# Solving 16x16 instead of 8x8 diagonal blocks on VectorE in the triangular inverse of a gated DeltaNet kernel

## The reference

```python
kb = kc * bc[..., None]
lower = jnp.tril(jnp.einsum('...id,...jd->...ij', kb, kc) * decay, -1)
a_mat = lower + jnp.eye(c, dtype=f32)
rhs = jnp.concatenate([vc * bc[..., None], kb * jnp.exp(gcum)[..., None]], axis=-1)
sol = lax.linalg.triangular_solve(a_mat, rhs, left_side=True, lower=True, unit_diagonal=True)
...
attn = jnp.einsum('...id,...jd->...ij', qc, kc) * decay
def step(s, xs):
    u_i, w_i, attn_i, qg_i, kg_i, gl_i = xs
    v_new = u_i - jnp.einsum('nhck,nhkv->nhcv', w_i, s)
    o = jnp.einsum('nhck,nhkv->nhcv', qg_i, s) + jnp.einsum('nhij,nhjv->nhiv', attn_i, v_new)
    s = s * gl_i[..., None, None] + jnp.einsum('nhck,nhcv->nhkv', kg_i, v_new)
    return s, o
```

## Time and profile before

| | us |
|---|---|
| median of 3 runs | 2033.04 (2029.34 to 2043.89) |
| profiled execution, its own time | 2042.09 |
| span of the profiled execution | 2040.3 |
| PE busy | 1976.5 (97%) |
| DVE busy | 1246.1 (61%) |
| ACT busy | 730.2 (36%) |
| POOL busy | 669.0 (33%) |

### The profile page before, as it was taken

The page is one execution under the profiler, slowest core; times in us unless marked ns, Lnnn a source line. Parts: engine busy times, 40 slices in busy tenths (PEclk is TensorE's granted clock), DMA queues, the critical chain, the costliest instruction groups (busy, mean ns, idle before and its releaser), DMA issues.

```text
span 2040.3 us, 37269 instructions
## 1 busy us (share of the span) xinstructions
PE 1976.5 (97%) x15623; PEld 1923.1 (94%) x15623; DVE 1246.1 (61%) x2428; ACT 730.2 (36%) x1238; POOL 669.0 (33%) x636
## 2 busy tenths in 40 slices
PE   4999999999999999999999999999999999999997
PEld 3999999999999988889999999999999999999996
DVE  6556566656663435663533279999999954463334
ACT  5322322232222114553322155555555543342220
POOL 3022113212321212000311148888888840031110
PEclk9999999999999989999999999999999999999998
DMA  5312212122213335112443333333333222223332
GB/s 166 104 52 64 64 63 64 60 69 63 64 60 95 114 104 170 53 51 66 130 129 129 103 96 94 94 94 94 93 94 87 82 82 75 83 89 117 106 106 101
DMA packets 77545, 184.98 MB, mean 91 GB/s; under 512 B 26648, under 2 KB 31576, under 8 KB 77128
## 3 DMA queue, kind: packets, MB, share of 16 engines
q1 hardware_dynamic: 66672, 163.52, 26.6%
q0 software_dynamic: 3504, 9.63, 1.4%
q10 hardware_dynamic: 7200, 9.44, 1.3%
HBM read 163.50 MB, written 19.06 MB: 89 GB/s over the span
## 4 chain that ended last, share of the span: by engine, by line
PE 28%; POOL 15%; DVE 4%; issue 3%; DMA 1%; ACT 0%; POOLq 0%; DVEq 0%; SPq 0%
PE acc L558 25%; POOL arena L2202 14%; PE acc L631 2%; DVE full L1491 1%; DVE act_lo L1488 1%; DVE gp L1491 1%; DMA w_raw<-wt 1%; POOL out_cfs L2455 1%; DVE w_lo L1488 1%; DVE arena L1488 1%; PE acc L586 1%; POOL out_cf L2454 0%; PE gp L601 0%; PE gp L610 0%; POOLq L2465 0%
## 5 line engine op out<-in xcount | busy, mean ns | idle before, releaser
L558 PE MATMUL acc<-act_hi,w_hi 128*128 128x288 f32 x3968 | 877.5, 303 | 4.8 <-DVE arena L1491 2.6
L558 PE MATMUL acc<-act_hi,w_lo 128*128 128x288 f32 x3968 | 851.9, 296 | 0.0
L558 PE MATMUL acc<-act_lo,w_hi 128*128 128x288 f32 x3968 | 851.5, 296 | 0.0
L558 PEld LDWEIGHTS acc<-act_hi,w_hi 128*128 128x128 f32 x3968 | 636.8, 190 | 24.2 <-issue 16.6
L558 PEld LDWEIGHTS acc<-act_hi,w_lo 128*128 128x128 f32 x3968 | 641.3, 189 | 0.0
L558 PEld LDWEIGHTS acc<-act_lo,w_hi 128*128 128x128 f32 x3968 | 641.2, 189 | 0.0
L2202 POOL TENSOR_TENSOR arena<-arena 128x512 f32<-128x512 f32 (+1 forms) x268 | 386.2, 1441 | 338.4 <-ACT arena L1321 285.5
L1488 DVE TENSOR_TENSOR w_lo<-w_raw,w_hi 128x1024 fp32r<-128x1024 f32 x266 | 394.3, 1505 | 31.7 <-ACT w_hi L1040 30.7
L1040 ACT ACTIVATE w_hi<-w_raw 128x1024 fp32r<-128x1024 f32 x266 | 276.1, 1052 | 363.2 <-PE acc L558 242.7
L1491 DVE SCALAR_TENSOR_TENSOR gp<-arena,par,gp 128x64 f32<-128x64 f32 (+1 forms) x688 | 248.0, 441 | 0.0
L1040 ACT ACTIVATE arena<-arena,par 128x512 f32<-128x512 f32 x240 | 166.7, 721 | 172.3 <-POOL arena L2202 118.3
(11 more groups left out here) (259 smaller groups left out, 1733.5 us busy)
## 6 DMA issues: line engine op xcount, KB each, us to landing
w_raw<-wt SPq DMA_DIRECT2D x266, 512.0 KB, 3.9
full<-x SPq DMA_DIRECT2D x8, 576.0 KB, 9.7
arena<-x SPq DMA_DIRECT2D x16, 288.0 KB, 3.6
arena<-x_scratch SPq DMA_DIRECT2D x16, 288.0 KB, 2.8
out_y<-full ACTq DMA_DIRECT2D x32, 144.0 KB, 1.9
x_scratch<-full ACTq DMA_DIRECT2D x14, 288.0 KB, 4.0
arena<-state_in SPq DMA_DIRECT2D x6, 512.0 KB, 4.2
out_sdn<-arena POOLq DMA_DIRECT2D x6, 512.0 KB, 3.2
```

The lines of the kernel that those rows point to most:

```text
L558: ins = pe.matmul(acc[:, s, i, 0:HALF], w[:, s, wk], a[:, k, i * HALF:(i + 1) * HALF], start=(k == 0 and j == 0), stop=(k == KT - 1 and j ...
```

## The change

`FIRST` becomes 4, so blocks are 16x16 and level 3 is gone: POOL's `L3`, PE's `a3` and `x3`, ACT's `A3`, DVE's `X3` and `T3`. `solve` has 14 rounds instead of 6. POOL's `B` is gone; a new DVE step `blk` masks the diagonal blocks instead, reading from the matrix only the 32x32 squares on its diagonal, with one instruction for each 32 partitions (4 for a head, 2 for the sampled tokens), and `mc` reduces these. PE's steps from a4 on keep their slots, and slots 11 and 12 hold no step any more. POOL's `L4` and `L5` now wait for `Mt` only and stand at slots 7 and 8; before, `L4` waited for `mc` and `L5` for `a3`.

```diff
-LEVELS, FIRST = 7, 3
+LEVELS, FIRST = 7, 4
...
-PE_PLAN |= {11 + i: n for i, n in enumerate(PE_HEAD[4:-1])}
+PE_PLAN |= {13 + i: n for i, n in enumerate(PE_HEAD[4:-1])}
...
-DVE_PLAN = {1: ["kg"], 2: ["dmask"], 3: ["ssum"], 4: ["vs", "Mt", "attn"], 6: ["mc", "solve", "Xt", "X"]}
+DVE_PLAN = {1: ["kg"], 2: ["dmask"], 3: ["ssum"], 4: ["vs", "Mt", "attn"], 5: ["blk", "mc", "solve", "Xt", "X"]}
...
-          "Mtb": "gcum", "attn": "gcum", "mc": "low", "solve": "low", "Xt": "low",
+          "Mtb": "gcum", "attn": "gcum", "blk": "gcum", "mc": "gcum", "solve": "low", "Xt": "low",
...
-POOL_PLAN = {0: ["scalars", "gB"], 3: ["nrm", "rn", "bn", "bp"], 4: ["B"], 7: ["L3"], 8: ["L4"]}
-POOL_PLAN |= {PE_AT[f"a{l - 2}"] + 1: [f"L{l}"] for l in range(5, LEVELS)} | {30: ["f1", "f2", "f3", "f4", "f5"]}
+POOL_PLAN = {0: ["scalars", "gB"], 3: ["nrm", "rn", "bn", "bp"], 7: ["L4"], 8: ["L5"]}
+POOL_PLAN |= {PE_AT[f"a{l - 2}"] + 1: [f"L{l}"] for l in range(6, LEVELS)} | {30: ["f1", "f2", "f3", "f4", "f5"]}
...
+            def diagonal_blocks(quad, m, rows):
+
+                for lo in range(0, rows, 32):
+                    q = slice(lo, lo + 32)
+                    ins = tt(quad[q], m[q, :, q], per_group(cst[q, C_BLK + lo:C_BLK + lo + 32], m.shape[1]), MUL)
+                return ins
+
...
+                elif name == "blk":
+                    dve.wait_ge(dve_h.sem, dve_h.at("Mt", it))
+                    ins = diagonal_blocks(quad_h, mt, P)
                 elif name == "mc":
-                    dve.wait_ge(pool_h.sem, pool_h.at("B", it))
-                    ins = dve.tensor_reduce(mc_h, mtl[0].rearrange("p c (b j) -> p c j b", j=BLOCK), AX_X, ADD)
+                    dve.wait_ge(dve_h.sem, dve_h.at("blk", it))
+                    ins = dve.tensor_reduce(mc_h, quad_h.rearrange("p c (b j) -> p c j b", j=BLOCK), AX_X, ADD)
...
-                elif name == "B":
-                    dv("Mt")
-                    ins = tt(mtl[0], mt, per_group(cst[:, C_BLK:C_BLK + P], 4))
                 elif name[0] == "L":
                     l = int(name[1])
-                    dv("Mt" if l == 3 else "mc")
+                    dv("Mt")
```

More of the change, by code:

```diff
@@ L103 @@
 assert LEVELS == 7
-DVE_HEAD = (["kg", "dmask", "ssum", "vs", "Mt", "attn", "mc", "solve", "Xt", "X"]
+DVE_HEAD = (["kg", "dmask", "ssum", "vs", "Mt", "attn", "blk", "mc", "solve", "Xt", "X"]
             + [n for i in LV for n in [f"X{i}"] + [f"T{i}"] * (i in IN_BLOCKS)]
@@ L108 @@
 ACT_HEAD = ["sq", "decay"] + [f"A{i}" for i in LV] + [f"q{c}" for c in range(1, NC)] + ["osq"]
-POOL_HEAD = (["scalars", "gB", "nrm", "rn", "bn", "bp", "B"] + [f"L{i}" for i in LV]
+POOL_HEAD = (["scalars", "gB", "nrm", "rn", "bn", "bp"] + [f"L{i}" for i in LV]
              + ["f1", "f2", "f3", "f4", "f5"])
 PE_PLAN = {1: "kv_tok", 2: "gcum", 3: "norm", 4: "gram"}
-PE_PLAN |= {11 + i: n for i, n in enumerate(PE_HEAD[4:-1])}
+PE_PLAN |= {13 + i: n for i, n in enumerate(PE_HEAD[4:-1])}
 def counts(names):
@@ L130 @@
 SPE = counts([n if h is None else f"{n}{h}" for g in SAMP_PLAN for n, h in g])
-SD = counts(["kg", "ssum", "vs", "dmask", "dmask2", "Mt", "Mtb", "attn", "mc", "solve", "Xt"]
+SD = counts(["kg", "ssum", "vs", "dmask", "dmask2", "Mt", "Mtb", "attn", "blk", "mc", "solve", "Xt"]
             + [f"{s}{h}" for g in range(H // 2) for s, h in (("r", g), ("vp", g), ("o", g), ("S", 2 * g), ("S", 2 * g + 1))]
@@ L134 @@
 SA = counts(["sq", "decay"] + [f"{s}{g}" for g in range(H // 2) for s in ("ks", "q")] + ["osq"])
-SP_ = counts(["gB", "nrm", "rn", "bn", "bp", "B"] + [f"vx{h}" for h in range(H)]
+SP_ = counts(["gB", "nrm", "rn", "bn", "bp"] + [f"vx{h}" for h in range(H)]
              + ["f1", "f2", "f3", "f4", "f5"])
@@ L401, in hybrid_step @@
         vps = rs_
-        z_h, mc_h, row_h, prod_h = (arena[:, 10364 + 32 * i:10396 + 32 * i].rearrange("p (c t) -> p c t", t=BLOCK)
+        z_h, mc_h, row_h, prod_h = (arena[:, 10364 + 64 * i:10428 + 64 * i].rearrange("p (c t) -> p c t", t=BLOCK)
                                     for i in range(4))
-        z_s, mc_s, row_s, prod_s = (arena[0:NS, 3840 + 64 * i:3904 + 64 * i].rearrange("p (h t) -> p h t", t=BLOCK)
+        quad_h = arena[:, 10620:10748].rearrange("p (c t) -> p c t", t=32)
+        z_s, mc_s, row_s, prod_s = (arena[0:NS, 3840 + 128 * i:3968 + 128 * i].rearrange("p (h t) -> p h t", t=BLOCK)
                                     for i in range(4))
@@ L410, in hybrid_step @@
                                   for i in range(3))
-        mtb_s = arena[0:NS, 4352:4864].rearrange("p (h t) -> p h t", h=H)
+        quad_s = arena[0:NS, 4352:4608].rearrange("p (h t) -> p h t", h=H)
         attn_s = arena[0:NS, 10364:10876].rearrange("p (h t) -> p h t", h=H)
@@ L1831, in samp_dve_step @@
                     ins = tt(attn_s, wide(1), dec_s, MUL)
+                elif name == "blk":
+                    own("Mtb")
+                    ins = diagonal_blocks(quad_s, mt_s, NS)
                 elif name == "mc":
-                    dve.wait_ge(samp_pool, SP_["B"])
-                    ins = dve.tensor_reduce(mc_s, mtb_s.rearrange("p h (b j) -> p h j b", j=BLOCK), AX_X, ADD)
+                    own("blk")
+                    ins = dve.tensor_reduce(mc_s, quad_s.rearrange("p h (b j) -> p h j b", j=BLOCK), AX_X, ADD)
                 elif name == "solve":
@@ L2352, in samp_pool_step @@
                     ins = tt(bp_s, bn_s, kq(nrm_s, 0))
-                elif name == "B":
-                    pool.wait_ge(samp_dve, SD["Mtb"])
-                    ins = tt(mtb_s, mt_s, per_group(cst[0:NS, C_BLK:C_BLK + NS], H))
                 elif name[0:2] == "vx":
```

## The result

The changed kernel took 2076.46 us (median of 4 runs, 2071.65 to 2084.43), the kernel before 2038.47 beside it: ratio 1.018, 95% interval 1.014 to 1.022. A second set gave 2073.71 against 2040.66, ratio 1.0156, interval 1.012 to 1.019. So the change costs 32 to 37 us on the 2033 of the median before. The profiled execution took 2071.65 (span 2069.8), 29.6 more than the one of before.

A forecast was written before the change was run, and what follows sets the result against it. PE, 97% busy, was taken to bound the kernel, with DVE's solve hidden without slack. Eight heads at 3.3 us (26.4) plus sampled tokens 6.5 made 33 us on 2033: 2066 us, range 2048 to 2080.

The forecast's parts named there:

- X to X4: DVE in each head: two weight halves, four taps and X4 take 5.74 us, X4 ending at 279.31.
- a5, set by PE's low clock: Third head: low clock costs PE 1.6 us, so a5 is due at 280.1, later than DVE's 279.4.
- st of the sampled tokens, more than that: PE's st at the sampled tokens starts 4.9 us late, waiting for DVE's longer solve.
- low clock behind st: Sampled tokens: the clock's fall raises st's lateness from 4.9 to 6.5 us.
- Slack: Before a3 in the heads: DVE's solve has no slack, X and slot 11's last matmul pair both ending at 267.10.
- turn-taking: DVE and POOL take turns whole on SBUF, so blk begins at 260.70, not 259.45; sharing would cost 1.2 us a head less.
- rounds: DVE's solve in the heads: fourteen rounds at 0.67 us take 9.4 us, ending at 271.95.
- Rival 2: Heads: blk does not wait for L5, everything 1.2 us earlier; 2048 to 2056 us; chance 0.13.
- rival 3: Heads: the solve stays hidden and PE keeps its 12.6 us; 2020 or 2025 us; chance 0.05.
- The clock: PE behind the wait ahead of a4: granted clock falls, costing 1.6 us of work each time.
- Rival 1: PE's clock stays high after the waits; 25 us added, 2058 us; chance 0.15.
- What PE saves: Dropping a3 and x3 takes 1.57 us a head off PE, 12.6 us in all 8.

The follow-up runs named there:

- e1: Changed kernel with POOL's mask L5 waiting for Xt instead of Mt; ratio to the kernel before 1.013.
- e12: Changed kernel with the weight half between attn and blk split at slot 2 instead; ratio to the kernel before 1.013.
- e2: Changed kernel with only the first 6 of the solve's 14 rounds, blocks not fully inverted; ratio to the kernel before 0.994.
- e4: Changed kernel with X4 and T4 moved to slot 12, plus 24 unused matmuls on PE ahead of a4's wait in each head; ratio to the kernel before 1.015.
- e3: Changed kernel with X4 and T4 moved from slot 14 to slot 12 of DVE's order; ratio to the kernel before 1.024.
- e5: Changed kernel with 24 unused matmuls on PE ahead of a4's wait in each head; ratio to the kernel before 1.015.
- e9: Changed kernel with sampled tokens at 8x8, L4 and L5 behind Xt, slot 4's weight half at slot 2, slot 12's behind X4; ratio to the kernel before 0.999.

## Why the prediction was right

The forecast was a median of 2066 us, the medians measured are 2076.46 and 2073.71. Of the distance, 8 to 10 us, some 5 to 8 lie in the base: the kernel before came out at 2038.47 and 2040.66 beside them, not at 2033.04. The 33 us that I added stand against 38.0 in one set and 33.1 in the other (differences of the medians). By its own steps, in the clock of before (third head, measured minus 5.66):

| step | predicted | measured |
|---|---|---|
| blk waits for L5 until | 260.70 | 260.68 |
| blk ends | 261.86 | 261.72 |
| mc | 0.4 | 0.29 |
| first round | 262.55 | 262.35 |
| 14 rounds | 9.4 | 9.55 |
| X ends | 273.57 | 273.52 |
| wait ahead of a4 | 3.4 | 3.37 |
| X to X4 | 5.74 | 5.73 |
| a5, set by PE's low clock | 280.1 | 279.91 |
| more a head | 3.3 | 3.15 (period) |
| 8 heads | 26.4 | 24.5 (679.7 - 655.2) |
| st of the sampled tokens, more than that | 4.9 | 4.7 (713.31 - 684.13 = 29.2) |
| low clock behind st | 1.6 | 4.9 |
| sum | 33 | 32 to 37 (ratios), 29.5 (profile's spans) |

- **Slack, turn-taking, rounds.** All three held, the second shown twice (e1, e12), the third by e2. Rival 2 (no wait for L5) and rival 3 (the solve stays hidden) are out.
- **The clock.** That it falls behind such a wait was right, and 1.6 us was near the 1.5 that e4 against e3 shows. Rival 1 is out, but what it would have saved is only 0.68 us a head (period of e5), near the 0.7 that I wrote (3.3 against 2.6).
- **What PE saves** was put at 1.57 a head and is 1.80 by e2. "No slack" was right but for 0.2 us, by which a3 already waited for X. I took the end of its last pair, 267.10, as the time when it could start, but a4 of the kernel before starts at 272.02, with its last pair ending at 272.09. It moves nothing in the sum, since a4's start is set by X.
- **The low clock behind st was mis-sized.** I took the price from a wait in the middle of dense matmuls. Behind st come 32 matmuls of 16 columns and long weight loads: PE is busy in the profile and still granted 0.50. Windows of the kernel after:

```profile
712.00:716.00 4.00, 2.69 (x14) 2.69 (x14) 3.46 (x5) 0.00 (x0) 0.00 (x0) 0.70 0.38 110
716.00:720.00 4.00, 4.00 (x21) 4.00 (x20) 0.00 (x0) 0.00 (x0) 0.00 (x0) 0.50 0.99 345
720.00:724.00 4.00, 4.00 (x18) 4.00 (x18) 0.00 (x0) 0.38 (x1) 0.00 (x0) 0.52 0.19 74
```

  The step behind st is 34.0 us later than before (724.94 - 690.90), so the low stretch cost 34.04 - 29.18 = 4.9 us. In this execution 7.6 us came back before the output projection (994.18 - 967.81 = 26.4), because the kernel before had three falls at later st groups and this execution had none. Windows of the kernel before:

```profile
728.00:732.00 4.00, 4.00 (x29) 4.00 (x29) 0.93 (x1) 0.38 (x1) 0.55 (x1) 0.76 0.81 262
732.00:736.00 4.00, 4.00 (x18) 4.00 (x18) 0.00 (x0) 0.00 (x0) 0.00 (x0) 0.50 0.63 184
```

  In the second profile of the changed kernel they were back. Of the 29.5 us between the profiles' spans the last 3 arise behind the start of the output projection and are not traced. So the mechanism of the heads was right, but that the sum came out near the measured one is in part luck: these terms cancel, and the range had no term for them.

## What to carry to other kernels

Before work is moved from a busy engine to an idle one, find the row where the idle one hands over: here X ended as a3 started, so the idle time of DVE (39% of the span) was worth nothing, and each microsecond added to a chain of dependent small instructions, beyond the 3 us that the dropped level left it, went to PE. Then clear the chain: an independent instruction standing in front of its first step, and another engine's masks that take turns with that step, cost 3.0 us a head here (e9), beside 5.75 us for the eight added rounds (271.81 to 277.56). An order on an in-order queue is changed one step at a time, with the question what stands behind the step that will now wait.

## What the runs showed of the hardware that was not expected

- TensorE's clock falls where PE is busy by the profile: st groups of 16-column matmuls were granted 0.50 for 4 us and more, and whether a given group was, changed between two executions of one kernel (three falls, some 9 us).
- A wait of 2.27 us ahead of a4 (e1) was followed by a granted clock of 1.00 in the third head, and one of 2.29 us in the fourth by 0.72 and 0.85 (344 to 352). Six of the eight heads show a fall in that kernel, and five in e12, with a wait of 2.15 in the third head. At that length the fall is not a property of the wait alone; at 3.37 us it came in all 8 heads.
- DVE's reduction of 512 values ran in 1.04 us beside POOL's masks, which held up a product of 128 values on 32 partitions for the whole rest of a mask (1.11 us).
- Four products on four different groups of 32 partitions took 1.16 us, and 0.28 us is one of the size: they don't overlap.
